# Output projection of the second block: recurrence half as split products, with the retention transposes inside its last quarter

## The chip, the cores and the metric

The kernel runs on one core of a Trainium2 chip. The metric is the device time of one execution in microseconds; 0.2% of it, about 3 us, is what a measurement can tell from no change. TensorE does the matrix products, VectorE, ScalarE and GpSimd the elementwise work, SyncE issues nearly all transfers. In the rows they are PE, DVE, ACT, POOL and SP.

## The reference

A token sequence of 256 rows of 1024 numbers goes through two blocks. The first block (two layers of attention and routed experts) is not touched by the change. The second block computes, per token:

```
u      = rms_norm(h) ; x_lru, g_lru, q, k, v, g_ret = split(u @ w_in)
y_lru  = rms_norm(recurrence(conv(x_lru)) * gelu(g_lru)) * lru_norm_gain        # 512 features
y_ret  = head_norm(retention(rotary(q), rotary(k), v)) * silu(g_ret)            # 512 features
h      = h + concat(y_lru, y_ret) @ w_out                                       # 1024 x 1024
u      = rms_norm(h)
h      = h + (gelu(a) * v) @ ffn_down,   a, v = split(conv(u @ ffn_up))         # 1024 -> 6144 -> 1024
out    = rms_norm(h)
```

All is fp32. The change is to the product with w_out: its upper 512 rows (the recurrence half) multiply y_lru, its lower 512 (the retention half) y_ret.

## The kernel before

Each engine has its program written out by hand, in one fixed order, and they meet by semaphores; there is no planner. The order around the change is thus the order of the lines in each engine's block.

**Two ways to multiply.** A plain fp32 matmul of a 128x128 by a 128x512 tile appears in the trace as two MATMUL records. A split product replaces it by three matmuls in the type fp32r: each operand is cut into a high part (a cast by ScalarE) and a low part (the value less its high part, a subtraction by VectorE or GpSimd), and high*high, high*low and low*high are summed in the same bank. Before the change the chunks of w_in, the retention half of w_out and the feed-forward weights are multiplied in this way; the recurrence half of w_out is plain (`project_out` with `recurrence_tile`, L963 to L976).

**The stages of the second block, in TensorE's order.** The six chunks of w_in (L1517 to L1541, products in `split_products`, L1064); within the last chunk, after its first half, four matmuls that sum the squares of the recurrence (L1538 to L1540). Then the eight transposes of queries and keys per token tile (`transposes("rqk")`, L1544, helper line L871), which wait for VectorE's rotation; scores (L1547, L1548), values (L1556 to L1558); the recurrence half of the output projection (L1560, L1561, matmuls at L971); the transposes of the retention's result (L1563, again L871); the retention half (`project_retention`, L996 to L1010, matmuls at L1006), into the same four banks (two token tiles t, two column halves n). After its third quarter stand the transposes of the next normed input for t = 0 (`beside`, L888). Then the feed-forward products (L1572, L1574, L1600) to the end.

**VectorE** in that stage: the low parts of the last w_in tiles (L2180) and the copy out of a bank (L2094); the rotation, `rope`, of twelve operations on 128x512 tiles that all read two tiles in SBUF (L565 to L570, called at L2622), which ends in `V_ROPE`; L2094 and L2626; copies of transposes (L2055), a reciprocal (L2101), the decay times scores (L2632); the normed recurrence LX in four tiles (L2635), the last of which gives `V_OUT`; statistics and norm of the retention (L2641 to L2656), ending in `V_RET`; eight low parts of w_out rows (L2660); two low parts of the transposed retention (L2664); three low parts of the first feed-forward weights (L2669); then the additions to the residual (`add_half`, L2112), which release ScalarE's squares (L1698) and with them the next norm.

**ScalarE**: the high parts of w_in (L1801) and copies out of banks (L1682); the root of the recurrence's mean square (L1690); half of the copies of transposes (L1638); eight high parts of w_out rows (L1963), two before and six after `V_OUT`; the high parts of the transposed retention (L1977); the first three feed-forward weights (L1985).

**GpSimd**: twelve low parts of w_in (L759), one product (L847), two loads of norm rows; then it has nothing until the feed-forward stage (L857).

**SyncE** loads w_out (two items of 2 MB, `I_OUT2`) as soon as two slots of the ring are free; the feed-forward weights follow in the ring.

Of the kernel before, what the change touches and what calls it, by code (L numbers as in the profile page):

```python
# [15 lines left out]
P = 128  # L16
# [104 lines left out]
def bass_two_blocks(nc, x, w_in, w_uq, w_ukv, w_o, w_qkv, na_bias, w_o2, ln_rows, rows, cols, w_route,  # L121
                    w_gate, w_up, w_down, w_in2, gates, w_out2, ffn_up, ffn_down, table, table2, out):
    with ExitStack() as ctx:
# [14 lines left out]
        def part(name, over, at, shape):  # L138

            return nc.alloc_sbuf_tensor_at(name, shape, F32R, offset=offset[over] + 4 * at)  # L140
# [196 lines left out]
        V_CONV, V_TANH, V_SQUARES, V_ROPE = LRU_T, LRU_T + 1, LRU_T + 2, LRU_T + 3  # L337
        V_OUT, V_RET = V_ROPE + RET_HEADS + 1, V_ROPE + RET_HEADS + 2
        E_SUM = LRU_T + 1
# [17 lines left out]
        def slot(i, a, b):  # L357
            return ring[:, i % RING, 0:a * b].rearrange("p (a b) -> p a b", b=b)
# [109 lines left out]
        def arrived(i):  # L468
# [5 lines left out]
                        [P, 512])[:, :] for k in range(2 * RET_HEADS)]  # L474
        RHI, RLO = part("ret_high", "arena", 13312, [P, RET_HEADS, SEQ]), part("ret_low", "arena", 1024, [P, RET_HEADS, SEQ])
        EVEN_ROWS, EVEN_MIXED = 2 * A_HEADS, 2
        EVEN_HIGH = [part(f"even_out_high{k}", "arena", 512 * k, [P, 512])[:, :] for k in range(EVEN_ROWS)]
# [7 lines left out]
        ROWS_FIRST = 2  # L485
        RET_FROM, RET_LOW_FROM = EVEN_ROWS + 2 * C, EVEN_ROWS + 2 * C - ROWS_FIRST

        def ret_row(k):
            return slot(I_OUT2[k // RET_HEADS], C, 512)[:, LRU_T + k % RET_HEADS, :]

        def out_high(n, c):
# [257 lines left out]
        def _(pool):  # L749
# [100 lines left out]
            pool.wait_ge(r_gain, 1)  # L850
            norm_rows(5)

            for g in range(DOWN_T):
# [7 lines left out]
        def _(pe):  # L861
# [97 lines left out]

            def recurrence_tile(c, t):  # L960
                return LX[:, c, t * P:(t + 1) * P]

            def project_out(g0, i, rows=range(C), tile=mixed_tile, beside=None, first=0, final=C - 1):  # L963
# [14 lines left out]
            def project_out_split(beside):  # L978

                for t in range(T):  # L980
                    tok = slice(t * P, (t + 1) * P)
                    for n in range(2):
                        pe.wait_ge(pj_free[t], G_OO + n - 1)
                        for c in range(C):
                            if t == 0 and n == 0:
                                pe.wait_ge(a_o, B_HEADS // 2 + c + 1)
                            if t == 0:
                                pe.wait_ge(*out_row_split(n, c))
                            for k, (a, b) in enumerate(((OHI, OUT_HIGH), (OHI, OUT_LOW), (OLO, OUT_HIGH))):
                                last = nc.tensor.matmul(bank[(G_OO + n) % 2 * 2 + t][:, :], a[:, c, tok], b[n][c],  # L990
                                                        start=(c == 0 and k == 0), stop=(c == C - 1 and k == 2))
                        last.then_inc(pj_done, 1)
                        if (t, n) == (T - 1, 0):
                            beside()

            def project_retention(beside):  # L996
# [562 lines left out]

            pe.wait_ge(by_vector, V_OUT)  # L1560
            project_out(G_OUT2, I_OUT2, range(LRU_T), recurrence_tile)  # L1561
            pe.wait_ge(by_vector, V_RET)
            transposes("yr", lambda b, t: YR[:, t, b * P:(b + 1) * P])  # L1563
            transposed("yr")
# [59 lines left out]
        def _(act):  # L1624
# [330 lines left out]
            high_tiles(S_IN2, [5 * TILES - 1])  # L1955
            next_tiles(S_IN2, 4, lambda: evac_2(4))
            evac_2(5)
            root(LI[:, 0, :])
# [8 lines left out]
            act.wait_ge(by_vector, V_SQUARES)  # L1967
            high_ret_rows(range(2))
            act.wait_ge(by_vector, V_OUT)
            high_ret_rows(range(2, 6))  # L1970
# [20 lines left out]
            act.wait_ge(by_vector, V_OUT)  # L1991
            act.wait_ge(tr_done, sum(TR["yr"]))
            for k in range(WBUF):
                high_weights(k)
# [43 lines left out]
        def _(dve):  # L2038
# [595 lines left out]
            for c in range(LRU_T):  # L2634
                last = v.scalar_tensor_tensor(LX[:, c, :], LX[:, c, :], COLS[:, Q_LN + c:Q_LN + c + 1], LI[:, 1, :],  # L2635
                                              ALU.mult, ALU.mult)
            last.then_inc(by_vector, 1)
            for h in range(RET_HEADS):
# [18 lines left out]
            last.then_inc(by_vector, 1)  # L2657
            for k in range(2 * RET_HEADS):
                dve.wait_ge(o_hi, RET_FROM + k + 1)
                v.tensor_tensor(RET_LOW[k], ret_row(k), RET_HIGH[k], ALU.subtract).then_inc(o_lo, 1)  # L2660
            for g, copied in enumerate((tr_act, tr_dve)):
                k = TR["yr"][0] + g
                dve.wait_ge(m_hi, EVEN_MIXED + C_HEADS // 2 + g + 1)
                v.tensor_tensor(RLO[:, 2 * g:2 * g + 2, :], bank[4 + k % 4][:, :].rearrange("p (a b) -> p a b", b=SEQ),  # L2664
                                RHI[:, 2 * g:2 * g + 2, :], ALU.subtract).then_inc(copied, 1)

            def low_weights(k):
# [142 lines left out]
```

## Time and profile before

| | before |
|---|---|
| median of 3 runs | 1484.53 us (1483.81 to 1484.76) |
| the profiled execution | 1488.51 us, its span 1486.4 us |
| TensorE busy | 1452.9 us, 98% of the span |
| VectorE, ScalarE, GpSimd busy | 559.9, 472.9, 150.4 us |
| mean granted clock of TensorE | 0.998 |

The span runs from the first to the last instruction; 2.1 us of the profiled execution's own time lie around it. Window limits and start times are microseconds from the span's start. Idle time of an engine matters only where the chain of work that ended last passes through it.

### The profile page before, as it was taken

Reading aid. Unit: us, or ns where it says so; the run is one execution under the profiler, and the core shown is the slowest. Engines: PE = TensorE matmul, PEld = TensorE weight load, DVE = VectorE, ACT = ScalarE, POOL = GpSimd, SP = SyncE. Lnnn points to the kernel's source line nnn. Section 1 sums busy time; section 2 is a strip of 40 time slices with the busy share of each in tenths; the row PEclk is TensorE's granted clock in tenths of the full one; section 3 lists DMA queues with packets and bytes.
Section 4 is the critical chain, followed back from the end, with each engine's and each line's share of the span. In section 5 each row is a group of like instructions: output and inputs, shape, how many; then the busy total and the mean of one; then the engine's idle time right before and its main releaser. Section 6 shows DMA issues by size and latency. Waiting matters only on the chain.

```text
span 1486.4 us, 19397 instructions
## 1 busy us (share of the span) xinstructions
PE 1452.9 (98%) x7786; PEld 885.1 (60%) x7786; DVE 559.9 (38%) x1162; ACT 472.9 (32%) x838; POOL 150.4 (10%) x136
## 2 busy tenths in 40 slices
PE   8999999999999999999999999999999999999998
PEld 6766544544544445987545445444453786888886
DVE  6775111111111113047211211111111588689965
ACT  4561111111111113454111111111111572676654
POOL 0211000000000002962000000000000710001200
PEclk9999999999999999999999999999999999999999
DMA  8658999999999999838999999999999846554410
GB/s 307 246 235 303 407 421 429 427 426 428 428 428 428 425 423 389 309 122 350 404 412 429 428 427 428 427 426 429 426 425 409 325 170 227 186 211 170 174 53 29
DMA packets 82597, 503.35 MB, mean 339 GB/s; under 512 B 5200, under 2 KB 10960, under 8 KB 55632
## 3 DMA queue, kind: packets, MB, share of 16 engines
q1 hardware_dynamic: 81792, 497.67, 82.4%
q0 software_dynamic: 576, 4.19, 0.7%
q8 instruction: 65, 1.06, 0.3%
q10 hardware_dynamic: 144, 0.26, 0.0%
q14 instruction: 20, 0.16, 0.0%
HBM read 501.05 MB, written 1.05 MB: 338 GB/s over the span
## 4 chain that ended last, share of the span: by engine, by line
PE 87%; DMA 6%; DVE 3%; ACT 2%; issue 1%; SPq 1%; POOL 0%; DVEq 0%; ACTq 0%
PE bank L1212 27%; PE bank L1259 14%; PE bank L1064 9%; PE bank L1157 8%; PE bank L1572 6%; DMA ring<-in_w_up 4%; PE bank L1600 4%; PE bank L1171 3%; PE bank L1574 3%; PE bank L971 2%; PE bank L990 2%; PE bank L908 1%; DMA ring<-in_w_in 1%; PE bank L1227 1%; PE bank L1095 1%
## 5 line engine op out<-in xcount | busy, mean ns | idle before, releaser
L1212 PE MATMUL bank<-ring,arena 128*64 128x512 f32 x1280 | 281.9, 596 | 6.2 <-issue 4.0
L1212 PEld LDWEIGHTS bank<-ring,arena 128*64 128x64 f32 x1280 | 94.9, 138 | 188.1 <-issue 186.9
L1212 PE MATMUL bank<-arena 128*64 128x512 f32 x576 | 167.8, 592 | 0.0
L2278 DVE TENSOR_TENSOR arena<-arena,bank 128x512 f32<-128x512 f32 x32 | 22.0, 688 | 370.5 <-PE bank L1212 370.5
L1259 PE MATMUL bank<-ring,arena 128*64 128x512 f32 x640 | 141.7, 595 | 2.4 <-ACT arena L1760 2.4
L1572 PE MATMUL bank<-x_split,w_high 128*128 128x512 f32 (+1 forms) x408 | 138.7, 391 | 0.2 <-DVE x_split L2081 0.2
L1157 PEld LDWEIGHTS bank<-SEL,x_by_row 128*128 128x128 f32 x1024 | 116.7, 192 | 25.8 <-issue 24.3
L2297 DVE SCALAR_TENSOR_TENSOR y_low<-bank,ST,y_high 128x512 fp32r<-128x512 f32 x64 | 48.0, 751 | 202.5 <-ACT y_high L1764 202.5
L1157 PE MATMUL bank<-SEL,x_by_row 128*128 128x128 f32 x1024 | 122.8, 278 | 0.0
L1764 ACT ACTIVATE y_high<-bank,ST 128x512 fp32r<-128x512 f32 x64 | 44.0, 687 | 245.7 <-PE bank L1259 245.7
L1212 PEld LDWEIGHTS bank<-arena 128*64 128x64 f32 x576 | 54.8, 137 | 106.3 <-issue 106.3
L1574 PE MATMUL bank<-x_split,w_low 128*128 128x256 f32 (+1 forms) x408 | 111.8, 274 | 0.0
L2669 DVE TENSOR_TENSOR w_low<-ring,w_high 128x1024 fp32r<-128x1024 f32 x72 | 96.4, 1341 | 30.6 <-ACT w_high L1985 30.2
L759 POOL TENSOR_TENSOR qkv_low<-ring,qkv_high 128x1024 fp32r<-128x1024 f32 x24 | 57.2, 2403 | 458.7 <-DVE X L2127 452.9
L1757 ACT COPY arena<-bank 128x512 f32<-128x512 f32 x30 | 17.6, 586 | 253.6 <-PE bank L1157 253.6
L1259 PEld LDWEIGHTS bank<-ring,arena 128*64 128x64 f32 x640 | 45.9, 137 | 84.2 <-issue 84.2
L1572 PEld LDWEIGHTS bank<-x_split,w_high 128*128 128x128 f32 x408 | 76.7, 188 | 17.2 <-DVE x_split L2081 0.3
L1259 PE MATMUL bank<-arena 128*64 128x512 f32 (+1 forms) x276 | 85.1, 590 | 0.0
L1212 PE MATMUL bank<-first_over_features,arena 128*64 128x512 f32 x192 | 84.4, 592 | 0.0
L1985 ACT CAST w_high<-ring 128x1024 fp32r<-128x1024 f32 x72 | 75.5, 1052 | 25.9 <-PE bank L1600 25.9
L1574 PEld LDWEIGHTS bank<-x_split,w_low 128*128 128x128 f32 x408 | 77.2, 189 | 0.0
L759 POOL TENSOR_TENSOR in_low<-ring,in_high 128x1024 fp32r<-128x1024 f32 x12 | 28.5, 2404 | 451.6 <-ACT in_high L1801 448.3
(387 smaller groups left out, 2213.0 us busy)
## 6 DMA issues: line engine op xcount, KB each, us to landing
ring<-in_w_gate SPq DMA_DIRECT2D x32, 2048.0 KB, 25.5
ring<-in_w_up SPq DMA_DIRECT2D x32, 2048.0 KB, 22.5
ring<-in_w_down SPq DMA_DIRECT2D x32, 2048.0 KB, 22.7
arena<-in_w_gate SPq DMA_DIRECT2D x18, 2048.0 KB, 21.6
arena<-in_w_down SPq DMA_DIRECT2D x16, 2048.0 KB, 23.7
arena<-in_w_up SPq DMA_DIRECT2D x14, 2048.0 KB, 16.5
ring<-in_ffn_up SPq DMA_DIRECT2D x12, 2048.0 KB, 9.0
ring<-in_w_in SPq DMA_DIRECT2D x8, 2048.0 KB, 15.6
```

Source lines behind the costliest of these rows:

```text
L759: nc.gpsimd.tensor_tensor(low, src, high, ALU.subtract).then_inc(w_lo, 1)
L1064: last = nc.tensor.matmul(part_(bank[g % 2 * 2 + t]), a, b, start=(part_ is parts[0] and c == 0 and n == 0), stop=(part_ is parts[-1] and ...
L1157: last = nc.tensor.matmul(bank[6 + c // 4][:, c % 4 * P:(c % 4 + 1) * P], x_rows(t, c), SEL[:, t, :], start=(t == 0), stop=(t == T - 1))
L1171: last = nc.tensor.matmul(bank[2 * t + half][:, :], SWT[:, t, :], y[:, 512 * half:512 * half + 512], start=False, stop=False, skip_group_c ...
L1212: last = nc.tensor.matmul(bank[4 + m][64 * e:64 * e + 64, :], XG[:, c, 64 * e:64 * e + 64], w[e][:, c, :], start=(c == 0), stop=(c == C - 1))
L1259: last = nc.tensor.matmul(bank[6 + half][64 * e:64 * e + 64, to], HT[:, j, 64 * e:64 * e + 64], rows_, start=(j == 0), stop=(j == FE // P ...
L1572: nc.tensor.matmul(bank[f % 4][:, :].rearrange("p (a b) -> p a b", a=2)[:, :, a:b], WHI[f % WBUF][:, c, :], XSPLIT[:, :, c, a:b], start=(a ...
L1574: last = nc.tensor.matmul(bank[f % 4][:, a:b], WLO[f % WBUF][:, c, :], XHI[:, c, a:b], start=False, stop=(b == SEQ and c == C - 1), skip_g ...
L1600: last = nc.tensor.matmul(bank[4 + 2 * t + half][:, :], a, w.rearrange("p a b -> p (a b)"), start=(c == 0 and n == 0), stop=(c == DOWN_T - ...
L1985: nc.scalar.copy(WHI[k % WBUF][:, :, :], src).then_inc(w_hi, 1)
L2297: v.scalar_tensor_tensor(YLO[:, cols_], bank[6 + half][:, :], slot_gate, YHI[:, cols_].bitcast(F32), ALU.mult, ALU.subtract).then_inc(s["y ...
L2669: v.tensor_tensor(WLO[k % WBUF][:, :, :], ffn_weights(k)[1], WHI[k % WBUF][:, :, :], ALU.subtract)\
```

## The change

- The recurrence half becomes split products: `project_recurrence` runs, for each token tile t and column half n, 4 x 3 matmuls in fp32r, 48 in all, in place of the 16 plain ones.
- The high parts of the upper rows of w_out are four ScalarE casts of 128x1024 (`REC_HIGH`), placed between two copies out of banks; the fourth waits for the sum of squares (`E_SUM`), since its buffer is read by it. The low parts are four GpSimd subtractions of 128x1024 (`REC_LOW`), each as soon as its high part is there. They then run while VectorE does the rotation.
- The high parts of the normed recurrence are four ScalarE copies of 128x256, each after its tile of LX; the low parts are four VectorE subtractions of 128x256, in place over LX, ahead of the retention's statistics. `V_OUT` keeps its meaning.
- The transposes of the retention's result move from after the recurrence half into its last quarter (t = 1, n = 1), after three of its twelve matmuls.
- VectorE does three of the eight low w_out rows before the low parts of the transposed retention, and five after, where all eight came before.
- ScalarE waits for the end of the recurrence half before the first feed-forward weights, since their buffers held `REC_HIGH`.
- No transfer is added, removed or moved.

```diff
@@ -335,7 +335,9 @@
         lru_g, lru_a = sem("lru_gates"), sem("lru_decay")
         by_vector, by_pe = sem("recurrence_by_vector"), sem("recurrence_by_pe")
         V_CONV, V_TANH, V_SQUARES, V_ROPE = LRU_T, LRU_T + 1, LRU_T + 2, LRU_T + 3
-        V_OUT, V_RET = V_ROPE + RET_HEADS + 1, V_ROPE + RET_HEADS + 2
+        V_NORMED = V_ROPE + RET_HEADS
+        V_OUT = V_NORMED + LRU_T
+        V_RET = V_OUT + LRU_T + 1
         E_SUM = LRU_T + 1
         E_SCORE, E_OUT = E_SUM, E_SUM + RET_HEADS
         part_used, parts_loaded = sem("part_of_slot_used"), sem("parts_of_slot_loaded")
@@ -473,6 +475,11 @@
         RET_LOW = [part(f"ret_out_low{k}", "ring", I_OUT2[k // RET_HEADS] % RING * SLOT + 512 * (LRU_T + k % RET_HEADS),
                         [P, 512])[:, :] for k in range(2 * RET_HEADS)]
         RHI, RLO = part("ret_high", "arena", 13312, [P, RET_HEADS, SEQ]), part("ret_low", "arena", 1024, [P, RET_HEADS, SEQ])
+        REC_AT = (0, 1024, 6144, 8192)
+        REC_HIGH = [part(f"recurrence_out_high{k}", "arena", at, [P, 2, 512]) for k, at in enumerate(REC_AT)]
+        REC_LOW = [part(f"recurrence_out_low{k}", "ring", I_OUT2[k // 2] % RING * SLOT + 1024 * (k % 2), [P, 2, 512])
+                   for k in range(4)]
+        LXHI, LXLO = part("recurrence_high", "XT", 0, [P, LRU_T, SEQ]), part("recurrence_low", "arena", 2048, [P, LRU_T, SEQ])
         EVEN_ROWS, EVEN_MIXED = 2 * A_HEADS, 2
         EVEN_HIGH = [part(f"even_out_high{k}", "arena", 512 * k, [P, 512])[:, :] for k in range(EVEN_ROWS)]
         EVEN_LOW = [part(f"even_out_low{k}", "ring", I_EO[k // A_HEADS] % RING * SLOT + 512 * (k % A_HEADS), [P, 512])[:, :]
@@ -483,10 +490,15 @@
             return slot(I_EO[k // A_HEADS], C, 512)[:, k % A_HEADS, :]
 
         ROWS_FIRST = 2
-        RET_FROM, RET_LOW_FROM = EVEN_ROWS + 2 * C, EVEN_ROWS + 2 * C - ROWS_FIRST
+        REC_FROM = EVEN_ROWS + 2 * C
+        RET_FROM, RET_LOW_FROM = REC_FROM + len(REC_AT), EVEN_ROWS + 2 * C - ROWS_FIRST
+        REC_MIXED = EVEN_MIXED + C_HEADS // 2
 
         def ret_row(k):
             return slot(I_OUT2[k // RET_HEADS], C, 512)[:, LRU_T + k % RET_HEADS, :]
+
+        def rec_rows(k):
+            return slot(I_OUT2[k // 2], C, 512)[:, k % 2 * 2:k % 2 * 2 + 2, :]
 
         def out_high(n, c):
 
@@ -849,6 +861,10 @@
             last.then_inc(r_gain, 1)
             pool.wait_ge(r_gain, 1)
             norm_rows(5)
+            for k in range(len(REC_AT)):
+                pool.wait_ge(o_hi, REC_FROM + k + 1)
+                nc.gpsimd.tensor_tensor(REC_LOW[k][:, :, :], rec_rows(k), REC_HIGH[k][:, :, :], ALU.subtract)\
+                    .then_inc(o_lo_first, 1)
 
             for g in range(DOWN_T):
                 f = g + DOWN_T
@@ -957,9 +973,6 @@
             def mixed_tile(c, t):
                 return MT[:, c, t * P:(t + 1) * P]
 
-            def recurrence_tile(c, t):
-                return LX[:, c, t * P:(t + 1) * P]
-
             def project_out(g0, i, rows=range(C), tile=mixed_tile, beside=None, first=0, final=C - 1):
 
                 for t in range(T):
@@ -992,6 +1005,30 @@
                         last.then_inc(pj_done, 1)
                         if (t, n) == (T - 1, 0):
                             beside()
+
+            def project_recurrence(beside):
+
+                for t in range(T):
+                    tok = slice(t * P, (t + 1) * P)
+                    for n in range(2):
+                        first = t == 0 and n == 0
+                        pe.wait_ge(pj_free[t], G_OUT2 + n - 1)
+                        kinds = ((LXHI, REC_HIGH), (LXHI, REC_LOW), (LXLO, REC_HIGH))
+                        order = [(c, m) for c in range(LRU_T) for m in range(2)] + [(c, 2) for c in range(LRU_T)] if first \
+                            else [(c, m) for c in range(LRU_T) for m in range(3)]
+                        for c, m in order:
+                            if t == 0 and m == 0 and c % 2 == 0:
+                                pe.wait_ge(o_lo_first, ROWS_FIRST + 2 * n + c // 2 + 1)
+                            if first and m == 0:
+                                pe.wait_ge(m_hi, REC_MIXED + c + 1)
+                            if first and m == 2:
+                                pe.wait_ge(by_vector, V_OUT + c + 1)
+                            a, b = kinds[m]
+                            last = nc.tensor.matmul(bank[(G_OUT2 + n) % 2 * 2 + t][:, :], a[:, c, tok],
+                                                    b[2 * n + c // 2][:, c % 2, :], start=(c == 0 and m == 0), stop=False)
+                            if (t, n, c, m) == (T - 1, 1, 0, 2):
+                                beside()
+                last.then_inc(by_pe, 1)
 
             def project_retention(beside):
 
@@ -1557,10 +1594,13 @@
                 nc.tensor.matmul(b[:, P:SEQ], RS[:, h, P:SEQ], v[0], start=True, stop=False)
                 nc.tensor.matmul(b[:, P:SEQ], RS[:, h, SEQ:DEC_W], v[1], start=False, stop=True).then_inc(by_pe, 1)
 
-            pe.wait_ge(by_vector, V_OUT)
-            project_out(G_OUT2, I_OUT2, range(LRU_T), recurrence_tile)
-            pe.wait_ge(by_vector, V_RET)
-            transposes("yr", lambda b, t: YR[:, t, b * P:(b + 1) * P])
+
+            def retention_transposes():
+
+                pe.wait_ge(by_vector, V_RET)
+                transposes("yr", lambda b, t: YR[:, t, b * P:(b + 1) * P])
+
+            project_recurrence(retention_transposes)
             transposed("yr")
             project_retention(lambda: transposes_by_token("n2", XN, xn_ready, 0, [0]))
 
@@ -1954,6 +1994,16 @@
             evac_2(3)
             high_tiles(S_IN2, [5 * TILES - 1])
             next_tiles(S_IN2, 4, lambda: evac_2(4))
+            def high_rec_rows(ks):
+
+                for k in ks:
+                    act.wait_ge(*arrived(I_OUT2[k // 2]))
+                    nc.scalar.copy(REC_HIGH[k][:, :, :], rec_rows(k)).then_inc(o_hi, 1)
+
+            act.wait_ge(by_vector, V_SQUARES)
+            high_rec_rows(range(3))
+            act.wait_ge(by_pe, E_SUM)
+            high_rec_rows([3])
             evac_2(5)
             root(LI[:, 0, :])
             evac_transposes("rqk", lambda b, n: RQK[:, b:b + n, :])
@@ -1966,6 +2016,9 @@
                 act.wait_ge(*arrived(I_OUT2[n]))
             act.wait_ge(by_vector, V_SQUARES)
             high_ret_rows(range(2))
+            for c in range(LRU_T):
+                act.wait_ge(by_vector, V_NORMED + c + 1)
+                nc.scalar.copy(LXHI[:, c, :], LX[:, c, :]).then_inc(m_hi, 1)
             act.wait_ge(by_vector, V_OUT)
             high_ret_rows(range(2, 6))
             root(var_h[:, :, :])
@@ -1990,6 +2043,7 @@
 
             act.wait_ge(by_vector, V_OUT)
             act.wait_ge(tr_done, sum(TR["yr"]))
+            act.wait_ge(by_pe, E_OUT + RET_HEADS + 1)
             for k in range(WBUF):
                 high_weights(k)
             for t in range(T):
@@ -2632,9 +2686,11 @@
                 v.tensor_tensor(RS[:, h, :], bank[4 + h][:, 0:DEC_W], KT2[:, L_DEC + h * DEC_W:L_DEC + (h + 1) * DEC_W],
                                 ALU.mult).then_inc(by_vector, 1)
             for c in range(LRU_T):
-                last = v.scalar_tensor_tensor(LX[:, c, :], LX[:, c, :], COLS[:, Q_LN + c:Q_LN + c + 1], LI[:, 1, :],
-                                              ALU.mult, ALU.mult)
-            last.then_inc(by_vector, 1)
+                v.scalar_tensor_tensor(LX[:, c, :], LX[:, c, :], COLS[:, Q_LN + c:Q_LN + c + 1], LI[:, 1, :],
+                                       ALU.mult, ALU.mult).then_inc(by_vector, 1)
+            for c in range(LRU_T):
+                dve.wait_ge(m_hi, REC_MIXED + c + 1)
+                v.tensor_tensor(LXLO[:, c, :], LX[:, c, :], LXHI[:, c, :], ALU.subtract).then_inc(by_vector, 1)
             for h in range(RET_HEADS):
                 dve.wait_ge(by_pe, E_OUT + h + 1)
                 for t in range(T):
@@ -2655,14 +2711,19 @@
             for t in range(T):
                 last = v.tensor_tensor(YR[:, t, :], YR[:, t, :], TOK[:, t, 1536:2048], ALU.mult)
             last.then_inc(by_vector, 1)
-            for k in range(2 * RET_HEADS):
-                dve.wait_ge(o_hi, RET_FROM + k + 1)
-                v.tensor_tensor(RET_LOW[k], ret_row(k), RET_HIGH[k], ALU.subtract).then_inc(o_lo, 1)
+            def low_ret_rows(ks):
+
+                for k in ks:
+                    dve.wait_ge(o_hi, RET_FROM + k + 1)
+                    v.tensor_tensor(RET_LOW[k], ret_row(k), RET_HIGH[k], ALU.subtract).then_inc(o_lo, 1)
+
+            low_ret_rows(range(3))
             for g, copied in enumerate((tr_act, tr_dve)):
                 k = TR["yr"][0] + g
-                dve.wait_ge(m_hi, EVEN_MIXED + C_HEADS // 2 + g + 1)
+                dve.wait_ge(m_hi, REC_MIXED + LRU_T + g + 1)
                 v.tensor_tensor(RLO[:, 2 * g:2 * g + 2, :], bank[4 + k % 4][:, :].rearrange("p (a b) -> p a b", b=SEQ),
                                 RHI[:, 2 * g:2 * g + 2, :], ALU.subtract).then_inc(copied, 1)
+            low_ret_rows(range(3, 2 * RET_HEADS))
 
             def low_weights(k):
                 dve.wait_ge(w_hi, K_FFN + k + 1)
```

## Rows read from the trace of the kernel before

**Rows 1.** The page: span, granted clock in 40 slices, feed-forward products.

```profile
span 1486.4 us, 19397 instructions
...
PEclk9999999999999999999999999999999999999999
...
L1572 PE MATMUL bank<-x_split,w_high 128*128 128x512 f32 (+1 forms) x408 | 138.7, 391 | 0.2 <-DVE x_split L2081 0.2
```

**Rows 2.** The chain that ended last, 1200 to 1300: start, duration, what.

```profile
1223.45 1.23 DVE in_low L2180
...
1232.18 5.48 PE bank L1064 x24
...
1245.80 13.73 PE bank L971 x32
...
1262.01 5.74 PE bank L1006 x24
```

**Rows 3.** Timeline, 1224 to 1240: start, duration, engine, line, operation [idle before].

```profile
1224.34 1.05 ACT L1801 CAST in_high<-ring 128x1024 fp32r<-128x1024 f32 x1 [0.75 <-PE bank L1064]
...
1227.10 0.74 DVE L2094 TENSOR_SCALAR arena<-bank,ST 128x512 f32<-128x512 f32 x1
...
1227.77 1.22 DVE L2180 TENSOR_TENSOR in_low<-ring,in_high 128x1024 fp32r<-128x1024 f32 x1
...
1228.90 0.69 DVE L565 TENSOR_TENSOR arena<-arena 128x512 f32<-128x512 f32 x1
...
1235.89 0.69 DVE L570 TENSOR_TENSOR arena<-arena 128x512 f32<-128x512 f32 x1
...
1236.31 0.69 ACT L1682 ACTIVATE arena<-bank,ST 128x512 f32<-128x512 f32 x1 [10.92 <-PE bank L1064]
...
1237.48 1.91 PE L871 MATMUL bank<-KT,arena 128*128 128x128 f32 x16
```

**Rows 4.** Timeline, 1243 to 1272: from the normed recurrence to the next norm.

```profile
1243.68 1.67 DVE L2635 SCALAR_TENSOR_TENSOR arena<-arena,COLS 128x256 f32<-128x256 f32 x4
...
1251.02 1.29 DVE L2656 TENSOR_TENSOR arena<-arena 128x512 f32<-128x512 f32 x2
...
1252.23 4.90 DVE L2660 TENSOR_TENSOR ret_out_low<-ring,ret_out_high 128x512 fp32r<-128x512 f32 x8
...
1259.37 1.04 PE L871 MATMUL bank<-KT,arena 128*128 128x128 f32 x8
...
1260.01 1.07 ACT L1977 CAST ret_high<-bank 128x512 fp32r<-128x512 f32 x2 [10.91 <-PE bank L871]
1260.63 1.29 DVE L2664 TENSOR_TENSOR ret_low<-bank,ret_high 128x512 fp32r<-128x512 f32 x2 [3.50 <-ACT ret_high L1977]
...
1262.06 3.50 DVE L2669 TENSOR_TENSOR w_low<-ring,w_high 128x1024 fp32r<-128x1024 f32 x3
...
1267.85 0.69 DVE L2112 SCALAR_TENSOR_TENSOR X<-X,bank 128x512 f32<-128x512 f32 x1 [1.70 <-PE bank L1006]
...
1271.16 1.09 PE L888 MATMUL bank<-KT,arena 128*128 128x128 f32 x8 [0.70 <-DVE arena L2171]
```

**Rows 5.** VectorE beside GpSimd: timelines at 99 and 1186, and line L2580's durations.

```profile
99.35 8.79 DVE L2507 TENSOR_TENSOR even_out_low<-ring,even_out_high 128x512 fp32r<-128x512 f32 x8
...
99.33 2.49 POOL L795 TENSOR_TENSOR arena<-arena,ST 128x512 f32<-128x512 f32 x2 [27.09 <-DVE ST L2504]
101.90 3.28 POOL L799 TENSOR_TENSOR arena<-arena,ROWS 128x512 f32<-128x512 f32 x2
...
1186.73 2.40 POOL L759 TENSOR_TENSOR in_low<-ring,in_high 128x1024 fp32r<-128x1024 f32 x1 [0.35 <-ACT in_high L1801]
...
L2580 DVE TENSOR_SCALAR arena<-arena,COLS x4: 400/409/2604, 1186.4 to 1189.5; 128x256 f32<-128x256 f32 x4
```

**Rows 6.** Busy time by stretch (PE, PEld, DVE, ACT, POOL), then granted clock, DMA.

```profile
498.70:502.10 3.40, 1.26 (x8) 0.34 (x6) 0.00 (x0) 0.60 (x1) 0.00 (x0) 1.00 1.02 434
502.10:505.50 3.40, 3.40 (x10) 1.20 (x8) 0.00 (x0) 0.00 (x0) 0.00 (x0) 0.50 0.98 419
```

## Prediction

> **What bounds the kernel now.** I read the page first: TensorE's slices are full, its clock is at the full level in all of them, and the feed-forward products, which fill the end of the span, waited 0.2 us in all for anything [rows 1]. So that last stage is TensorE alone, and whatever the change moves ahead of it arrives at the end one for one. Then the chain that ended last, around the change [rows 2]: VectorE's low parts at 1223, products of w_in, the plain recurrence half (13.73 us for 32 records) and the retention half. Then the timelines for who stands beside whom [rows 3, 4], and two stretches elsewhere that show what VectorE does beside GpSimd [rows 5] and what TensorE's clock does after a pause [rows 6]. The sum is made against the profiled execution (span 1486.4, own time 1488.51); the median of the runs, 1484.53, is 4.0 lower, and I put the difference on the median.
>
> **1. The products.** Gone: 13.73 us [rows 2]. Added: 48 matmuls in fp32r of the same shape as those of w_in, 24 of which take 5.48 us, 0.228 each [rows 2]: 10.96. Gain 2.8.
>
> **2. The transposes inside.** Before, the plain products end at 1245.80 + 13.73 = 1259.53 and the retention half begins at 1262.01 [rows 2]: 2.5 us for transposes, high and low parts. Now TensorE pays the transposes alone, 8 of them at 1.91/16 = 0.12 [rows 3], 0.95. The retention half would begin at 1245.80 + 10.96 + 0.95 = 1257.7, which is 4.3 earlier (products and transposes together). What covers the rest: the transposes start after 39 matmuls, at 1254.7. From their first to the end of the low parts took 1262.01 - 1259.37 = 2.6 before [rows 2, 4], so the low parts are there at 1257.3, in front of 1257.7. `V_RET` was at 1252.3 (end of L2656 [rows 4]); the four new subtractions of 128x256 ahead of it, about 0.4 each as L2635's [rows 4], make that 1253.9, 0.8 ahead of its need. If this cover is gone, every further microsecond is on the path. The three low rows, 3 x 0.61 (4.90/8 [rows 4]), end at 1255.8, about when the first high part is there. The high parts of LX lie in ScalarE's wait beside L2635 and cost nothing.
>
> **3. What is late next.** On VectorE five low rows, 3.0 us, now stand behind the low parts of the retention, and behind them the three first feed-forward weights (3.50 [rows 4]). Measured from the start of the retention half, VectorE is free at -0.4 + 3.0 + 3.45 = 6.1. The residual addition that releases the next norm stood at 1267.85 [rows 4], 5.8 from that start, with another addition done before it, at 1265.5. Now the two run together, the second from 6.1 + 0.6 = 6.7: 0.9 late. TensorE already waited 0.70 for that norm at L888 [rows 4], so there is no slack: loss 0.9. ScalarE's weights now wait for the end of the recurrence half; the three take 3 us from there and are ahead of VectorE's need at 2.6 to 6.1.
>
> Parts 1 to 3: -4.3 + 0.9 = **-3.4**.
>
> **4. The four high parts.** 4 x 1.05 us of ScalarE, in its idle time of 10.92 before L1682 [rows 3]. The fourth waits for the sum of squares, at about 1232.2; queued behind it is L1682, due at 1236.31: nothing. Without that gap it would cost 4.2.
>
> **5. The four low parts on GpSimd.** Their inputs are there from 1226.4 on (1224.34 and two casts of 1.05 [rows 3]), so they meet VectorE's rotation, 1228.90 to 1236.58, whose twelve operations all read two tiles in SBUF. What does this cost? At 99.35 VectorE ran eight such subtractions of 128x512 while GpSimd ran four operations of the same size: 8.79 us [rows 5], against 4.90 for the same eight alone [rows 4]. 3.89/4 = 0.97 lost per GpSimd operation, about its whole work, and GpSimd's own durations grew in turn: the two take turns, whole instructions at a time. At 1186.73 GpSimd did exactly the operation that is now added, and one of four VectorE operations took 2.604 us where the median is 0.409 [rows 5]: 2.2 lost, between operations that stood in an unbroken row. So GpSimd gets in between VectorE's operations. Price of each new subtraction: from 1.95 (twice 0.97, by size) to 2.4 (its whole duration), and below it nothing at all if the rotation were not touched. I take 2.2, from the row with the same GpSimd operation. 4 x 2.2 = 8.8, less 0.7 that lies beside L2094, which reads a bank, is 8.1. The rotation ended at 1236.58 and TensorE began its transposes at 1237.48 [rows 3], a slack of 0.9. So TensorE waits 7.2 more. The low part L2180 at 1227.77 gets 1.4 of that delay; its matmuls run only from 1234.9, so it costs nothing more. After the rotation the chain is as before, moved.
>
> The Trainium skill, "SBUF — State Buffer", section "Who interferes with whom", says that a VectorE instruction with two inputs in SBUF and a GpSimd instruction that reads SBUF exclude each other, and that the second to issue blocks fully until the first is through. By that rule the price would be the whole 2.4 us, part 5 would be 8.0 and the time 0.8 later than by the row.
>
> **6. The clock.** TensorE then stands idle from 1237.4 to 1244.7. At 499.7 it stood idle for about 2 us, busy 1.26 of 3.4, and the granted clock fell to 0.50, its 1.2 GHz level, for the next 3.4 us under full work, which costs 1.7 [rows 6]. An idle stretch more than three times as long should do the same. The 7.4 us of transposes, scores and values that follow would start at the low level. Bounds: nothing, if the clock stays, and 3.7, about two such low stretches of work. I take 2.1, a little over one.
>
> **Sum:** -3.4 + 7.2 + 2.1 = **+5.9**, 1490.4 us, 0.4% slower.
>
> **The rivals.**
> - *The rotation is not slowed* (the other side; it is also the case that GpSimd gets in only after it). Place: part 5. Then -3.4: 1481.1. For it: GpSimd has nothing else to do, its lows are needed only from 1246 on. Against: both places [rows 5]. It decides at (3.4 + 0.9 + 0.7)/4 = 1.25 us lost per subtraction: below that the change gains, and even the nearest lower row says 1.95. Chance 0.17.
> - *Contention, but the clock stays up*: -3.4 + 7.2 = +3.8, 1488.3. For it: the clock stayed at its full level all through this stretch, over a wait of 0.70 too [rows 1, 4]. Against: the fall after a far shorter pause [rows 6]. Chance 0.14.
> - *Two of the four get in*, at the pauses between the rotation's parts: 4.4 - 0.7 - 0.9 = 2.8, -0.6 in all, 1483.9. Against: VectorE's unbroken row at 1186 was entered. Chance 0.06.
> - *The clock stays low beyond values into the 11 us of products*: over 1493. Chance 0.05.
>
> **How the numbers follow.** The forecast has 0.58. With its bounds (1.95 to 2.4 per subtraction: 6.2 to 8.0; clock 0 to 3.7; parts 1 to 3) contention gives 1487.3 to 1492.9. The range goes down to 1483.5 for the two-of-four case and up to 1494.5 for part of the low-clock one; outside it is mostly the uncontended case. What a measurement can tell is 0.2%, 3.0 us. Slower by more: 0.58 + 0.12 + 0.05 = 0.75. Within it: 0.06 + 0.02 = 0.08. Faster: 0.17.
>
> **What would show it.** In the changed profile: L565 to L570 take 14 to 16 us rather than 7.7, with single operations near 2.8, and GpSimd's four subtractions among them; TensorE idle about 7 us, released by L570; the granted clock at 0.5 in one stretch after 1239; scores at twice their spacing. Right in any case: 48 products at 0.228, no gap before L1006, L888 waiting 1.6 rather than 0.7. Wrong, if rotation operations keep 0.69 beside GpSimd: then the time is near 1481. Wrong in size, if the clock does not fall, or if `V_RET` comes after the transposes' turn.

## The result and the profile after

| | before | after |
|---|---|---|
| median | 1484.80 us (1483.81 to 1487.78, 6 runs) | 1492.65 us (1490.21 to 1494.11, 6 runs) |
| ratio, 95% interval | | 1.0046 (1.0035 to 1.0056) |
| span of the profiled execution | 1486.4 us | 1490.4 us |
| mean granted clock | 0.998 | 0.996 |

The change makes the kernel 0.46% slower. The medians are 7.9 us apart; the ratio, taken over all the runs, is worth 6.8 us (5.2 to 8.3); the forecast was 5.9. All ratios compare fast runs alone, so two slow ones are left out below: one of 1624.74 us with the transposes behind again, and one of 7095.65 us of the kernel before that ran beside it.

Spans of single profiles are not a good measure here, since stages that the change does not touch differ by a microsecond or two between executions. So I compare one **stage** in all profiles: from the first matmul of the sum of squares (L1539 before) to the first feed-forward product (L1572 before). Before: 1230.29 to 1274.85, 44.56 us. After: 1229.33 to 1278.77, 49.44 us, 4.9 longer. A second profile of each gave 44.53 and 49.48.

The chain that ended last, after, 1200 to 1310 (start, duration, what); it answers to [rows 2]:

```profile
1226.92 2.63 DVE in_low L2234
1229.56 2.78 DVE arena L577
1232.34 2.80 DVE arena L578
1235.14 2.79 DVE arena L579
...
1243.78 3.29 PE bank L887 x16
...
1253.47 8.88 PE bank L1027 x39
1262.35 0.45 PE bank L887 x4
...
1275.09 1.09 PE bank L904 x8
```

Before, the chain passed from products of w_in through the copies of the transposes. Now it passes through the whole rotation on VectorE (L577 to L582, before L565 to L570). The transposes of queries and keys (L887 x16) take 3.29 us, not 1.91. Products of the recurrence are L1027.

The timeline after, 1224 to 1244 (start, duration, engine, line, operation [idle before]); it answers to [rows 3]:

```profile
1224.28 2.95 ACT L2001 CAST recurrence_out_high<-ring 128x1024 fp32r<-128x1024 f32 x3
...
1225.42 11.96 POOL L866 TENSOR_TENSOR recurrence_out_low<-ring,recurrence_out_high 128x1024 fp32r<-128x1024 f32 x4 [19.78 <-ACT recurrence_out_high L2001]
1226.13 0.75 DVE L2148 TENSOR_SCALAR arena<-bank,ST 128x512 f32<-128x512 f32 x1
1226.79 2.76 DVE L2234 TENSOR_TENSOR in_low<-ring,in_high 128x1024 fp32r<-128x1024 f32 x1
1229.48 2.86 DVE L577 TENSOR_TENSOR arena<-arena 128x512 f32<-128x512 f32 x1
1231.25 1.05 ACT L2001 CAST recurrence_out_high<-ring 128x1024 fp32r<-128x1024 f32 x1 [4.02 <-PE bank L1576]
1232.26 2.88 DVE L578 TENSOR_TENSOR arena<-arena 128x512 f32<-128x512 f32 x1
1235.07 2.86 DVE L579 TENSOR_TENSOR arena<-arena 128x512 f32<-128x512 f32 x1
1235.34 0.69 ACT L1722 ACTIVATE arena<-bank,ST 128x512 f32<-128x512 f32 x1 [3.04 <-PE bank L1101]
...
1237.85 0.68 DVE L580 TENSOR_TENSOR arena<-arena 128x512 f32<-128x512 f32 x1
...
1243.78 3.28 PE L887 MATMUL bank<-KT,arena 128*128 128x128 f32 x16 [7.11 <-DVE arena L582]
```

GpSimd's four subtractions fill 1225.4 to 1237.4. In that time VectorE does one operation that reads a bank at its old price (L2148, 0.75) and four that read two tiles in SBUF: 2.76 where it was 1.22, and three of 2.86 to 2.88 where they were 0.69. The next one (L580), after GpSimd's last, takes 0.68 again. TensorE waits 7.11 us for the end of the rotation.

The clock, in the view of busy time by stretch (PE, PEld, DVE, ACT, POOL, then granted clock, DMA share, GB/s), after:

```profile
1237.00:1244.00 7.00, 0.22 (x1) 0.22 (x2) 6.89 (x11) 0.00 (x0) 0.38 (x1) 0.69 0.90 313
1244.00:1248.00 4.00, 3.13 (x17) 2.92 (x16) 2.31 (x5) 2.25 (x5) 0.00 (x0) 0.69 1.05 388
```

It was at 0.5 (1.2 GHz) from 1239.7 to 1246.5, 6.83 us, of which 4.1 passed in the wait. Before, it was full through all of this [rows 1].

### The profile page after: what moved, and what is told of

Same layout as the page of the kernel before. It is cut to its first block, busy times and chain, and to the rows that moved or that the text cites. A ratio compares the mean times of both kernels' runs of the same rounds, so it can differ in the third digit from the quotient of the medians.

```text
span 1490.4 us, 19449 instructions
## 1 busy us (share of the span) xinstructions
PE 1451.1 (97%) x7802; PEld 889.2 (60%) x7802; DVE 569.3 (38%) x1166; ACT 478.2 (32%) x846; POOL 162.3 (11%) x140
## 3 DMA queue, kind: packets, MB, share of 16 engines
q0 software_dynamic: 576, 4.19, 0.7%
## 4 chain that ended last, share of the span: by engine, by line
PE 88%; DVE 5%; DMA 4%; ACT 2%; issue 1%; SPq 0%; POOL 0%; DVEq 0%; ACTq 0%
PE bank L1249 28%; PE bank L1296 14%; PE bank L1101 8%; PE bank L1194 8%; PE bank L1612 6%; PE bank L1640 4%; PE bank L1208 3%; PE bank L1614 3%; DMA ring<-in_w_up 2%; PE bank L1003 1%; PE bank L924 1%; DMA ring<-in_w_in 1%; PE bank L984 1%; PE bank L1264 1%; PE bank L1132 1%
```

## The experiments

Theory: the loss is GpSimd and VectorE excluding each other, 2.2 us for each subtraction, plus the clock that falls in the wait it makes; the split products and the moved transposes gain 3.4 us by themselves. Rivals: the loss sits in the new products, in the order on VectorE or ScalarE, or behind the stage. All ratios are to the kernel before, run beside each.

**All four low parts after the rotation.**

```diff
             norm_rows(5)
+            pool.wait_ge(by_vector, V_ROPE)
             for k in range(len(REC_AT)):
```

> The changed kernel, but GpSimd waits for the end of the rotation before its four low parts. Theory (GpSimd and VectorE exclude each other where both read SBUF): the twelve operations of the rotation are back at 0.6 each, TensorE's idle time of 7.1 us before the transposes is gone, the clock stays at its full level; the gain of 3.4 us of parts 1 to 3 shows, 1481. But the four low parts then end at about 1245 and the last meets the normed recurrence (L2689, two tiles in SBUF) at 1242.7: up to 2.2 of the 3.4 can be lost there, so 1481 to 1484. Rival (the loss is not contention, but comes from the split products, the moved transposes or the later weights): the time stays near the changed kernel's, 1490 to 1493.

Ratio 0.9991 (0.9982 to 1.0000), stage 42.51: 2.1 shorter than before, 6.9 shorter than with the change. The wait before the transposes is gone, the clock stays full in the stage. What is left of the loss, in VectorE's and GpSimd's timelines:

```profile
1237.83 0.41 DVE L2681 TENSOR_SCALAR arena<-bank 128x256 f32<-128x256 f32 x1
...
1239.52 1.74 DVE L2156 RECIPROCAL arena<-arena 128x256 f32<-128x256 f32 x1
1241.30 1.95 DVE L2687 TENSOR_TENSOR arena<-bank,arena 128x384 f32<-128x384 f32 x4
1243.16 2.96 DVE L2690 SCALAR_TENSOR_TENSOR arena<-arena,COLS 128x256 f32<-128x256 f32 x2
...
1236.14 9.31 POOL L867 TENSOR_TENSOR recurrence_out_low<-ring,recurrence_out_high 128x1024 fp32r<-128x1024 f32 x4 [30.05 <-DVE arena L582]
```

GpSimd now needs 9.31 for the four rather than 11.96: nobody makes it wait (2.34 to 2.36 each, against 2.83 to 3.35 in the changed kernel). Beside it, VectorE's operations with an input in a bank (0.41, 1.95 for four) and the reciprocal with one input in SBUF (1.74) take just what they took before. The first with two inputs in SBUF, the normed recurrence, meets the fourth low part: 2.96 for two, 2.1 more than alone. TensorE waits 1.0 for it. The rival is out.

**Two beside, two after.**

```diff
             for k in range(len(REC_AT)):
+                if k == 2:
+                    pool.wait_ge(by_vector, V_ROPE)
                 pool.wait_ge(o_hi, REC_FROM + k + 1)
```

> The changed kernel, but GpSimd does two low parts at once and the other two only after the rotation. Theory: the loss goes by the number of GpSimd operations that fall into the rotation, 2.1 to 2.3 us each: the rotation ends 4.4 - 0.7 = 3.7 later than alone, TensorE waits 2.8 of it, -3.4 + 2.8 = -0.6, about 1484, and 1.7 more if the clock falls in that wait. Rival (VectorE loses a fixed time once GpSimd is awake at all, or loses nothing): rotation as long as with four, or as long as with none.

Ratio 1.0005 (0.9996 to 1.0014), no difference shown; stage 43.75, 0.8 shorter than before, as expected (0.6).

VectorE's and GpSimd's timelines:

```profile
1225.14 2.78 DVE L2236 TENSOR_TENSOR in_low<-ring,in_high 128x1024 fp32r<-128x1024 f32 x1
1227.84 2.85 DVE L577 TENSOR_TENSOR arena<-arena 128x512 f32<-128x512 f32 x1
1230.61 0.68 DVE L578 TENSOR_TENSOR arena<-arena 128x512 f32<-128x512 f32 x1
...
1223.77 6.37 POOL L868 TENSOR_TENSOR recurrence_out_low<-ring,recurrence_out_high 128x1024 fp32r<-128x1024 f32 x2 [19.79 <-ACT recurrence_out_high L2003]
```

Two GpSimd operations, two long VectorE operations. The loss goes by the number of overlaps, against the fixed loss of the rival: 2.9 us of the stage for two (43.75 less the 40.81 of the run below without any). TensorE waited 2.7 us, and the clock did not fall.

**TensorE kept busy in the wait.**

```diff
-            pe.wait_ge(by_vector, V_ROPE)
             pe.wait_ge(lru_g, 4)
+            keep_clock(7, 8)
+            pe.wait_ge(by_vector, V_ROPE)
```

> The changed kernel, with eight plain matmuls of 128x512 on TensorE, whose result is not used, in its wait for the rotation. Theory (part 6 of the prediction): the granted clock stays at 1.0, the 16 transposes take 1.9 us rather than 3.3, and the time is 1.4 to 3.7 us shorter than the changed kernel's, with the contention's 7.1 us still there: 1488 to 1490. Rival (the low clock costs nothing, since the chain passes through VectorE at that time): no difference beyond 0.5 us.

Ratio 1.0028 (1.0018 to 1.0039), stage 48.11: 1.3 shorter than with the change (1.4 to 3.7 was expected of the time).

TensorE's timeline, with the unused products (L1132) ahead of the transposes:

```profile
1236.74 7.03 PE L1132 MATMUL bank<-KT 128*128 128x512 f32 x16
1244.00 1.97 PE L887 MATMUL bank<-KT,arena 128*128 128x128 f32 x16 [0.23 <-DVE arena L582]
```

The clock stayed full and the transposes take 1.97. So in that profile the low clock costs 1.3 us, all of it in the transposes (3.28 - 1.97). By the runs the gap between the two kernels is 1.0046 to 1.0028, 2.7 us, but their intervals overlap.

**Only the transposes moved, products plain.** `retention_transposes` is passed to `project_out` of the kernel before as `beside`, so it runs ahead of the last quarter; nothing else of the change is made.

```diff
-            project_out(G_OUT2, I_OUT2, range(LRU_T), recurrence_tile)
-            pe.wait_ge(by_vector, V_RET)
-            transposes("yr", lambda b, t: YR[:, t, b * P:(b + 1) * P])
+            def retention_transposes():
+
+                pe.wait_ge(by_vector, V_RET)
+                transposes("yr", lambda b, t: YR[:, t, b * P:(b + 1) * P])
+
+            project_out(G_OUT2, I_OUT2, range(LRU_T), recurrence_tile, beside=retention_transposes)
```

> The kernel before, with only the retention transposes moved ahead of the last quarter of the plain recurrence products. Theory: the wait of 1.6 us at the start of the retention half and the start latency go, the transposes' own 0.95 stay: 1.3 to 1.7 us faster, 0.1%. The new-order loss of 0.9 at L888 does not appear, since the low rows stay ahead of the low parts. Rival (the retention half was not bound by this wait): no difference.

Ratio 0.9985 (0.9975 to 0.9995), stage 42.68, 1.9 shorter, where 1.3 to 1.7 was expected. This half of the change is a gain alone, and the wait at the next norm stayed at 0.7, as expected.

**No overlap at all.** Three low parts after the rotation, the fourth after the low parts of the recurrence.

```diff
+            pool.wait_ge(by_vector, V_ROPE)
             for k in range(len(REC_AT)):
+                if k == 3:
+                    pool.wait_ge(by_vector, V_OUT + LRU_T)
                 pool.wait_ge(o_hi, REC_FROM + k + 1)
```

> The changed kernel, with three of GpSimd's low parts after the rotation and the fourth after the low parts of the recurrence, so that none meets a VectorE operation that reads two tiles in SBUF. Theory: no VectorE operation over 1.8 us between the rotation and the retention half; against the run with all four after the rotation, the 2.1 us of L2690 and TensorE's 1.03 us wait before the products go, and from the sum of squares to the first feed-forward product it is 3.2 to 3.6 us shorter than the kernel before (it was 2.05 shorter with all four): 1481, ratio 0.9975 to 0.9980. Rival (GpSimd also slows VectorE where one input is in a bank, or the fourth comes too late for the products, which need it at 1248.9 to 1249.4): 2 us shorter or less, and a wait on GpSimd inside the products.

Ratio 0.9981 (0.9972 to 0.9990), stage 40.81, 3.75 shorter than before (3.2 to 3.6 was expected); no wait on GpSimd in the products, and the first operation of the normed recurrence, 2.57 us in the run with all four after the rotation, takes 0.47. This is parts 1 to 3 of the prediction without the contention. Against the busy-TensorE run, which differs from it by the contention alone (and eight unused matmuls in the wait), the stage is 7.3 shorter.

**One weight after the additions, on top.**

```diff
-            for k in range(WBUF):
+            for k in range(WBUF - 1):
                 low_weights(k)
             for t in range(T):
                 for n in range(2):
                     add_half(G_OUT2, t, n, 1.0)
+                    if (t, n) == (0, 1):
+                        low_weights(WBUF - 1)
```

> As the run before it, and the third of the first feed-forward weights' low parts on VectorE comes after the two additions of token tile 0, not before. Theory (part 3 of the prediction): the wait of 1.65 us at the transposes of the next norm falls back to 0.70, 0.9 us more is gained, stage 4.1 to 4.5 us shorter than the kernel before. Rival (those additions are not what is late, but ScalarE's weights behind the end of the recurrence half): wait stays at 1.6.

Ratio 0.9977 (0.9967 to 0.9987), stage 39.80, 4.8 shorter than before and 1.0 shorter than the run above; 4.1 to 4.5 was expected, since the run above was expected to gain less than it did. It was profiled a second time, with 39.84. From the chain that ended last:

```profile
1244.16 8.88 PE bank L1030 x39
1253.04 0.87 PE bank L890 x8
1253.91 2.06 PE bank L1030 x9
1255.96 5.45 PE bank L1046 x24
```

And its timelines of VectorE, TensorE and GpSimd:

```profile
1262.24 1.23 DVE L2733 TENSOR_TENSOR w_low<-ring,w_high 128x1024 fp32r<-128x1024 f32 x1
...
1264.76 1.09 PE L907 MATMUL bank<-KT,arena 128*128 128x128 f32 x8 [0.64 <-DVE arena L2228]
...
1235.02 7.01 POOL L869 TENSOR_TENSOR recurrence_out_low<-ring,recurrence_out_high 128x1024 fp32r<-128x1024 f32 x3 [30.05 <-DVE arena L582]
1245.12 2.40 POOL L869 TENSOR_TENSOR recurrence_out_low<-ring,recurrence_out_high 128x1024 fp32r<-128x1024 f32 x1 [3.10 <-DVE recurrence_low L2696]
```

Products, transposes, the last nine products and the retention half stand without a gap, and the wait at the next norm is 0.64. It is the best version found, about 0.23% faster than the kernel before; it and the run above are not told apart by their intervals, only by their stages.

**The transposes behind again**, on the version without overlap.

```diff
-            project_recurrence(retention_transposes)
+            project_recurrence(lambda: None)
+            retention_transposes()
```

> As the first run of this call, but the retention transposes stand behind the recurrence products again. Theory: their start, the high and low parts are in the open again, 2.5 us instead of 0.95: stage 1.5 to 1.7 us longer than with them inside, and some of it back at the next norm, since VectorE's low rows and weights run on meanwhile. Rival (the low rows, not the transposes, bound the start of the retention half): no difference.

Ratio 0.9995 (0.9985 to 1.0004), stage 42.85, 2.0 longer than with them inside. The wait is back, in TensorE's timeline:

```profile
1256.87 0.47 PE L1046 MATMUL bank<-ret_out_high,ret_high 128*128 128x512 f32 x1 [1.61 <-DVE ret_low L2728]
```

The expectation was off in two points: the loss was 2.0 and not 1.5 to 1.7, and nothing came back at the next norm, whose wait was 1.83 rather than 1.62. VectorE's five low rows stand behind the low parts of the retention, so they are late with them instead of running on. Against the kernel before, this run has the split products alone: 1.7 shorter in the stage (44.56 less 42.85).

**VectorE does the four low parts itself**, after the rotation.

```diff
-            for k in range(len(REC_AT)):
-                pool.wait_ge(o_hi, REC_FROM + k + 1)
-                nc.gpsimd.tensor_tensor(REC_LOW[k][:, :, :], rec_rows(k), REC_HIGH[k][:, :, :], ALU.subtract)\
-                    .then_inc(o_lo_first, 1)
...
                 .then_inc(by_vector, 1)
+            for k in range(len(REC_AT)):
+                dve.wait_ge(o_hi, REC_FROM + k + 1)
+                v.tensor_tensor(REC_LOW[k][:, :, :], rec_rows(k), REC_HIGH[k][:, :, :], ALU.subtract)\
+                    .then_inc(o_lo_first, 1)
             evac_2(5)
```

> The changed kernel, with the four low parts by VectorE itself right after the rotation, nothing on GpSimd. Theory: the same subtraction costs VectorE 1.15 to 1.22 us when it does it and 2.1 to 2.2 when GpSimd does it beside VectorE, so this costs 4.7 instead of 8.1: the rotation ends where it did, the scores start about 4.5 later than before, the stage is about 1.0 to 1.5 us longer than before the change, 3.5 shorter than with the change, and 1.5 to 3 more if the clock falls in the wait for the copies. Rival (VectorE's queue, not GpSimd, is the limit): as slow as the changed kernel.

Ratio 1.0007 (0.9998 to 1.0016), stage 45.82: 1.3 longer than before, 3.6 shorter than with the change. The clock was low for 3.4 us, from 1243.1 on, just after TensorE's wait of 4.19 had ended: the scores took 4.39 us, where they took 2.70 before.

VectorE's timeline, and TensorE's where the scores begin:

```profile
1235.85 4.63 DVE L2676 TENSOR_TENSOR recurrence_out_low<-ring,recurrence_out_high 128x1024 fp32r<-128x1024 f32 x4
...
1242.93 1.11 PE L1580 MATMUL bank<-arena 128*128 128x256 f32 x2 [4.19 <-ACT arena L1674]
```

VectorE spends 4.63 on all four. Letting GpSimd do them beside it cost VectorE more than doing them (8.1). The expectation had the stage 1.0 to 1.5 longer with the clock up, and 1.5 to 3 more with a fall; with the fall it was 1.3. Two things were misjudged and nearly cancel: the scores started 3.3 later than before, not 4.5, mostly because VectorE had stood idle for 1.1 us after the rotation, and the low clock added 1.7.

**Second profiles.** Three kernels were profiled once more.

> The changed kernel once more, for a second profile. Open: the runs say 6.8 us slower, the profiled stage 4.9. Theory: the rest is the granted clock, which differs from execution to execution (means of 0.993 to 0.997): the low stretch at the rotation or those elsewhere are longer in other executions; from the sum of squares to the first feed-forward product 54.3 again within 1.5. Rival: a cost behind that stage, in the feed-forward products.

> The kernel before once more. From the first feed-forward product of the up part to the first of the down part the profiles show either 137.3 or 139.7 us, with pairs of products every 0.347 or 0.353 us. If this goes by the execution, the kernel before can show 137.3 here, where it showed 139.7; if it goes by the kernel, it shows 139.7 again.

> The best version once more (three low parts after the rotation, the fourth after the low recurrence, one weight after the additions). It showed 139.7 in the up part. By the execution: either value. By the kernel: 139.7 again. The stage before it 39.8 again within 0.3.

The changed kernel took 1489.98 beside 1484.97 for the kernel before, one run each: 5.0 apart. Its stage was 49.48 and its low clock at the rotation again 6.83 us long, so that stretch did not vary. (The 54.3 in the expectation is not the length of this stage, which had measured 49.44.) Its feed-forward products were faster, 137.3 rather than 139.7 us, so the rival's cost behind the stage did not show either. The kernel before and the best version showed 139.7 again, with stages of 44.53 and 39.84.

## Why the prediction was right

The sign and the mechanism held, and the size came out within the noise of the runs, in part by luck (below). Term by term, with what the stage shows:

- **Parts 1 and 2, products and transposes, -4.3.** 39 products took 8.88, 0.228 each, as priced. No gap before the retention half; `V_RET` came at 1261.3, 0.9 ahead of the transposes at 1262.19 (0.8 was forecast). With part 3: -3.75 measured without overlap, -3.4 forecast. The 0.35 more lies in the transposes, 0.87 rather than 0.95 in the open, and in the retention half, 5.45 us where it follows without a gap and 5.74 before [rows 2].
- **Part 3, +0.9.** The wait at the next norm went from 0.70 to 1.65, and moving one weight gave back 1.0. The place and the size are shown.
- **Part 4, nothing.** ScalarE's four high parts left 3.04 us of idle time before L1722.
- **Part 5, +7.2.** TensorE's wait was 7.11. Three overlaps cost VectorE 2.17 to 2.19 each (2.86 to 2.88 less 0.69), the first one 1.54 (2.76 less 1.22), since GpSimd's first subtraction lay in part beside L2148: 8.1 in all, as forecast. The row of the kernel before that I took, with the same GpSimd operation, had said 2.2; the half-size rows, doubled, would have said 1.95, and the page's rule, read as the whole duration of 2.4, a bit too much. The rule of the Trainium skill, "SBUF — State Buffer", section "Who interferes with whom", holds in its kind: GpSimd's operation too was longer by what was left of the VectorE operation ahead of it, and operations with at most one input in SBUF, which it leaves out of the contention unless they run in a 2-port mode (inputs in a bank, the reciprocal), kept their times beside GpSimd. But the row that gave the 2.2, L2580 [rows 5], is itself a TENSOR_SCALAR with one tile in SBUF and columns of scalars, and it was held up: 2.60 for 0.41. So two tiles in SBUF are not the whole condition, which the prediction did not notice; in which mode L2580 ran, no run shows. The price was right all the same.
- **Part 6, +2.1.** The clock fell as forecast, but in the profile it cost 1.3: the transposes ran at the low level, while the scores, forecast at twice their spacing, started at 1247.93 with the clock up again and kept it. This term was sized too high for the profiled execution. Its ground was weak, too: the fall after the pause at 499.7 [rows 6] came in 5 of the 13 profiles of this document only, though none of the kernels differs there (see the last section).

The stage's 4.9 splits into -3.75 + 7.3 + 1.3, from the stages of the run without overlap, the one with TensorE busy and the changed kernel. As differences of the same four stages they add up by themselves; what bears them out are the lines, 7.11 us of wait for the 7.3 and 1.31 us of slower transposes for the 1.3. The forecast's 5.9 is 1.0 above the stage, 0.8 of it from the clock. That it lies within the interval of the runs' 6.8, as the stage's 4.9 does not, is luck, since no term of it stands for what is missing between 4.9 and 6.8.

The rival without contention is out (rotation operations of 2.86), the one with the clock up as well, the one with the clock low into the products too (it was up from 1246.5 on, the products began at 1253.2), and so is the one in which GpSimd gets in only at the rotation's pauses: L577 to L579 follow each other without one, and GpSimd stood between all of them.

What stays open is the rest of the 6.8 us that the runs say. The mean clock of the changed kernel's six executions was 0.993 to 0.997, 0.996 in the profiled one, so others had longer low stretches; where, their means don't show. As an estimate: the mean of the six, 0.9947, is 15.9 us at half the clock, against 11.7 in the profiled execution; 4.2 us more would cost 2.1 at most, if TensorE were busy in all of it. That would be enough for the missing 1.9, but it is not shown. The single pair of runs that is 5.0 apart cannot decide it.

## What to carry to other kernels

A free engine is not free work: before giving GpSimd a subtraction, look for what VectorE does at that time, and whether it reads two tiles in SBUF; one operation with a single tile in SBUF was held up as well (L2580). Here an overlap cost VectorE 2.2 us, nearly twice what the work costs on VectorE itself (1.16); put beside operations that read a bank, and the reciprocal, the same four cost nothing. Price such an overlap from a place in the trace where the two already meet. And when work moves off the path, see which queue it now stands in: the low rows put behind the transposes cost 1 us at the next norm until one weight was moved too.

## What was not expected

The feed-forward products have two steady paces in profiles of the same instructions. From the first up product to the first down product it is 137.3 or 139.7 us; pairs of products start every 0.347 or 0.353 us, with the clock full in both. TensorE's timeline of the kernel before, 1321 to 1323:

```profile
1321.10 0.28 PE L1574 MATMUL bank<-x_split,w_low 128*128 128x256 f32 x1
1321.22 0.40 PE L1572 MATMUL bank<-x_split,w_high 128*128 128x512 f32 x1
1321.46 0.28 PE L1574 MATMUL bank<-x_split,w_low 128*128 128x256 f32 x1
```

and the version without overlap:

```profile
1321.00 0.28 PE L1617 MATMUL bank<-x_split,w_low 128*128 128x256 f32 x1
1321.11 0.39 PE L1615 MATMUL bank<-x_split,w_high 128*128 128x512 f32 x1
1321.34 0.28 PE L1617 MATMUL bank<-x_split,w_low 128*128 128x256 f32 x1
```

The changed kernel showed 139.7 in one profile and 137.3 in the other, so it goes by the execution. What sets the pace is open. Part of it comes back behind: from the first down product to the end it is 71.9 us in the seven profiles with 139.7 and 72.5 to 72.6 in the six with 137.3. So two spans can differ by 1.7 us by this alone, and the stage itself starts anywhere from 1227.7 to 1230.3, which is why the stage was compared here.

The clock's falls go by the execution as well. Near 500 us all 13 profiles have the same code and a pause of TensorE of 1.75 to 2.14 us. In five of them 3.41 us at half the clock follow (after 2.03 to 2.14 us); in eight none do, and four of these have pauses of 2.12 to 2.14, as long as the others'. Busy time by stretch (PE, PEld, DVE, ACT, POOL, then granted clock) of the kernel before and of the one with TensorE busy in the wait:

```profile
499.00:506.00 7.00, 4.86 (x16) 1.60 (x14) 0.00 (x0) 0.60 (x1) 0.00 (x0) 0.76 1.01 428
499.00:506.00 7.00, 4.86 (x24) 1.68 (x22) 0.00 (x0) 0.60 (x1) 0.00 (x0) 1.00 1.02 433
```

Beside the rotation a wait of 2.7 us (two low parts) was followed by no fall, one of 4.2 (VectorE's own low parts) and both of 7.1 (the changed kernel, twice) were. The length of the pause alone does not decide it, and one profile is not enough to price a fall after a short one.
